# Picking the first four experts' rows inside gate and up of expert 0 in a transformer block with 64 experts

## The reference

```python
N_GROUPS, EXPERTS_PER_GROUP, TOP_K_EXPERTS = 8, 8, 2
D_EXPERT = D_MODEL // 8                       # 256
def hier_moe(h, wg, bg, we, be, w_gate, w_up, w_down):
    ...
    g_prob = jax.nn.softmax((xt @ wg).astype(jnp.float32) + bg.astype(jnp.float32), axis=-1)
    g_p, g_idx = lax.top_k(g_prob, 1)
    ...
    e_in = jnp.take_along_axis(e_logits, g_idx[:, :, None], axis=1)[:, 0]
    e_val, e_loc = lax.top_k(e_in, TOP_K_EXPERTS)
    weight = (g_p * jax.nn.softmax(e_val, axis=-1)).astype(h.dtype)
    ...
    def expert_chunk(args):
        xc, e = args
        return (jax.nn.silu(xc @ w_gate[e]) * (xc @ w_up[e])) @ w_down[e]
```

## Time and profile before

| | before |
|---|---|
| median of three runs | 1948.68 us |
| profiled execution | 1948.38 us |
| its span | 1946.6 us |
| TensorE busy | 1871.2 us (96%) |
| VectorE busy | 705.6 us (36%) |
| ScalarE busy | 584.6 us (30%) |
| GpSimd busy | 245.3 us (13%) |
| HBM read | 495.88 MB |

### The profile page before, as it was taken

One profiled execution on the slowest core, in us unless ns is written; L12 is line 12 of the kernel. 1 busy time (PEld: TensorE's weight loads), 2 busy tenths in 40 slices (PEclk: granted clock), 3 DMA queues, 4 the chain that ended last, 5 costly groups with the idle time before them and its releaser, 6 DMA issues.

```text
span 1946.6 us, 28605 instructions
## 1 busy us (share of the span) xinstructions
PE 1871.2 (96%) x11936; PEld 1352.2 (69%) x11936; DVE 705.6 (36%) x1773; ACT 584.6 (30%) x1212; POOL 245.3 (13%) x208
## 2 busy tenths in 40 slices
PE   6999999999999999999999999989999899999997
PEld 6887777777777767788986666556665565656663
DVE  5331223333766668701042232322323222222222
ACT  5323333333443444422312232212212122121322
POOL 2433343433000000144100000000000000000000
PEclk9999999999999999999999999999999999999999
DMA  9554233234232232145489999999999999999995
GB/s 284 134 147 118 66 86 82 70 71 92 45 76 44 55 117 79 44 142 195 191 349 420 429 426 426 427 427 427 427 426 427 427 428 426 428 427 427 427 423 231
DMA packets 177745, 505.95 MB, mean 260 GB/s; under 512 B 52930, under 2 KB 136258, under 8 KB 151754
## 3 DMA queue, kind: packets, MB, share of 16 engines
q1 hardware_dynamic: 175306, 495.66, 66.5%
q0 software_dynamic: 2304, 8.39, 1.1%
HBM read 495.88 MB, written 16.53 MB: 263 GB/s over the span
## 4 chain that ended last, share of the span: by engine, by line
PE 81%; DMA 16%; ACT 1%; DVE 1%; issue 0%; SPq 0%; POOL 0%; POOLq 0%; ACTq 0%; DVEq 0%
PE banks L967 26%; PE banks L1375 13%; PE banks L1124 9%; PE banks L1400 8%; DMA x_region<-in_w_up 7%; DMA at_region<-in_w_up 7%; PE banks L1297 6%; PE banks L1376 3%; PE banks L1104 3%; PE banks L1076 2%; PE banks L1054 2%; PE banks L1346 2%; DMA ht_region<-in_w_up 2%; PE banks L1016 1%; PE banks L1215 1%; PE banks L1061 1%
## 5 line engine op out<-in xcount | busy, mean ns | idle before, releaser
L967 PE MATMUL banks<-ht_rounded,ring_rounded 128*128 128x512 f32 x1056 | 359.2, 394 | 0.7 <-ACT at_region L1538 0.7
L967 PEld LDWEIGHTS banks<-ht_rounded,ring_rounded 128*128 128x128 f32 x1056 | 195.1, 188 | 53.3 <-issue 13.8
L1375 PE MATMUL banks<-at_region,ht_region 128*64 128x256 f32 x800 | 179.0, 382 | 9.3 <-DMA at_region<-in_w_up 9.3
L864 POOL TENSOR_TENSOR ring_rounded<-ring_region,at_rounded 128x512 fp32r<-128x512 f32 (+1 forms) x92 | 115.9, 1291 | 511.3 <-ACT at_rounded L1477 511.3
L1376 PE MATMUL banks<-at_region,ht_region 128*64 128x256 f32 x768 | 175.3, 388 | 0.0
L2269 DVE SCALAR_TENSOR_TENSOR at_rounded<-banks,small,ring_rounded 128x512 fp32r<-128x512 f32 x128 | 96.1, 751 | 208.8 <-ACT ring_rounded L1763 207.9
L1763 ACT ACTIVATE ring_rounded<-banks,small 128x512 fp32r<-128x512 f32 x128 | 88.0, 687 | 241.3 <-PE banks L1400 241.3
L2262 DVE COPY consts<-banks 128x128 f32<-128x128 f32 x64 | 18.7, 292 | 388.1 <-PE banks L1385 388.1
L1375 PEld LDWEIGHTS banks<-at_region,ht_region 128*64 128x64 f32 x800 | 109.1, 138 | 67.3 <-issue 21.1
L967 PE MATMUL banks<-ht_rounded,at_rounded 128*128 128x512 f32 x352 | 142.7, 405 | 1.0 <-ACT at_region L1530 0.7
L1753 ACT ACTIVATE ring_region<-banks,consts 64x256 f32<-64x256 f32 x64 | 30.0, 469 | 364.4 <-PE banks L1376 364.1
(11 more groups left out here) (300 smaller groups left out, 3488.2 us busy)
## 6 DMA issues: line engine op xcount, KB each, us to landing
at_region<-in_w_gate SPq DMA_DIRECT2D x23, 2048.0 KB, 30.0
at_region<-in_w_up SPq DMA_DIRECT2D x22, 2048.0 KB, 27.6
at_region<-in_w_down SPq DMA_DIRECT2D x22, 2048.0 KB, 23.9
ring_region<-in_w_in SPq DMA_DIRECT2D x36, 1024.0 KB, 5.9
x_region<-in_w_down SPq DMA_DIRECT2D x17, 2048.0 KB, 26.6
x_region<-in_w_up SPq DMA_DIRECT2D x15, 2048.0 KB, 28.9
x_region<-in_w_gate SPq DMA_DIRECT2D x14, 2048.0 KB, 29.9
ring_region<-in_w_gate SPq DMA_DIRECT2D x9, 2048.0 KB, 32.6
```

What stands on the lines that cost most here:

```text
L864: ins = nc.gpsimd.tensor_tensor(w_low[n % RING][:, ks, 0:width], ring[n % RING][:, ks, 0:width], w_high[n % 2][:, ks, 0:width].bitcast(F32 ...
L967: ins = mm(out, w[:, k, 0:width], h[:, k, :], start=k == 0 and i == 0, stop=k == KT - 1 and i == 2)
L1375: mm(place[0:CAP, 0:D_EXPERT], x, gate[j], start=j == 0, stop=j == KT - 1)
```

## The change

- **Fillers**: 7, 1 and 2 products in place of 16, 4 and 6.
- **Pick matrix**: the half for experts 0 to 3 is built first, by itself, and signals a semaphore of its own, `first_picks`; then the half for experts 4 to 7 (`pick_ready`).
- **Picks**: four of the sixteen picks of the first half stand ahead of expert 0; pick j + 4 then stands ahead of gate and up of slice j. The four banks are 6, 2, 3 and 0, since bank 7 now takes gate and up of expert 0 at the same time.
- **Root products** of group 0 move from ahead of gate and up of expert 0 to behind them, ahead of `gu_done`.
- The copies on ScalarE and VectorE keep their order and count (`copy_first`). `FIRST_PARTS` has a single part, so `FIRST_MORE` is 0, and all later counts stay as they were.

```diff
+FIRST_PARTS = ((0, HALF),)
+FIRST_MORE = len(FIRST_PARTS) - 1
...
-        def half_places(g, h):
-            return (whole_banks if h or g else first_banks, TURN4)
+        first_places = ((banks[:, 6, :], banks[:, 2, :], banks[:, 3, :], banks[:, 0, :]), (banks[:, 2, :], banks[:, 3, :], banks[:, 0, :]))
...
             place_rows(0)
-            keep_busy(16)
+            keep_busy(7)
             pe.wait_ge(chosen_ready, 1)
...
-            keep_busy(4)
+            keep_busy(1)
             place_slots(0)
-            keep_busy(6)
+            keep_busy(2)
+
+            first_rows = xg[0].rearrange("r (p k) -> r k p", k=KT)
+
+            def pick_first(part, j):
+                lo, hi = FIRST_PARTS[part]
+                if j == 0:
+                    pe.wait_ge(first_picks, part + 1)
+                if part == 0 and j == 0:
+                    pe.wait_ge(idx_ready, 1)
+                    pe.wait_ge(xg_in[0], 16)
+                places = first_places[part]
+                at = j - len(places)
+                if at >= 0:
+                    pe.wait_ge(xT_v if at % 2 else xT_a, part * KT // 2 + at // 2 + 1)
+                mm(places[j % len(places)][:, 0:hi - lo], first_rows[:, j, :], pick[:, lo:hi], start=True, stop=True).then_inc(picked, 1)
...
-                if picks is not None:
+                if picks is not None and (g or e8 >= PER // 2):
                     i = max(j for j in range(KT) if TURN4[j] == 1)
                     pe.wait_ge(xT_v if i % 2 else xT_a, done + i // 2 + 1)
                 fence(c, g)
-                if e8 == 0:
+                def root_of_slots():
...
+                if e8 == 0 and not begins_all(c, g):
+                    root_of_slots()
                 for j in range(KT):
                     if picks is not None:
                         pe.wait_ge(xT_v if j % 2 else xT_a, done + j // 2 + 1)
...
+                    if begins_all(c, g) and e8 == 0 and j + len(first_places[0]) < KT:
+                        pick_first(0, j + len(first_places[0]))
...
+                if e8 == 0 and begins_all(c, g):
+                    pe.wait_ge(pick_ready, 1)
+                    ins = root_of_slots()
                 ins.then_inc(gu_done, 1)
...
-            pick_half(0, 0)
+            for j in range(len(first_places[0])):
+                pick_first(0, j)
...
-            build_pick(0, 0)
+            v.tensor_copy(group_slots, slot_of_row[:, 0:PER]).then_inc(own_slots, 1)
+            dve.wait_ge(own_slots, 1)
+            pick_by_slots = pick.rearrange("p (e s) -> p e s", e=PER)
+            for lo, hi in FIRST_PARTS:
+                es = slice(lo // CAP, hi // CAP)
+                v.tensor_tensor(pick_by_slots[:, es, :], bcast(iota, 1, es.stop - es.start),
+                                bcast(group_slots[:, es], 2, CAP), ALU.is_equal).then_inc(first_picks, 1)
+            es = slice(HALF // CAP, PER)
+            v.tensor_tensor(pick_by_slots[:, es, :], bcast(iota, 1, PER - es.start), bcast(group_slots[:, es], 2, CAP),
+                            ALU.is_equal).then_inc(pick_ready, 1)
```

More of the change, by code:

```diff
@@ L553, in picks_ahead, with half_after @@
         def picks_ahead(c, g):
-            return g * 2 * KT if fast(c) else (c * N_GROUPS + g) * KT + N_GROUPS * KT
+            return g * 2 * KT + (FIRST_MORE * KT if g else 0) if fast(c) else (c * N_GROUPS + g) * KT + N_GROUPS * KT + FIRST_MORE * KT
         def copies_ahead(c, g):
-            return g * KT if fast(c) else (c * N_GROUPS + g) * (KT // 2) + N_GROUPS * KT // 2
+            return g * KT + (FIRST_MORE * KT // 2 if g else 0) if fast(c) else ((c * N_GROUPS + g) * (KT // 2) + N_GROUPS * KT // 2
+                                                                               + FIRST_MORE * KT // 2)
+        def half_after(g, h):
+            return h * (KT // 2) + (FIRST_MORE * KT // 2 if h and not g else 0)
         def begins_all(c, g):
@@ L1279, in pick_half @@
             def pick_half(g, h):
                 pe.wait_ge(pick_ready, g + 1)
-                pe.wait_ge(idx_ready, 1)
-                pe.wait_ge(xg_in[g % 2], g // 2 * 16 + 16)
-                place, turn = half_places(g, h)
                 rows = xg[g % 2].rearrange("r (p k) -> r k p", k=KT)
+                if not h:
+                    pe.wait_ge(xg_in[g % 2], g // 2 * 16 + 16)
                 for j in range(KT):
-                    if (h or g) and j == TURN4.index(0):
+                    if j == TURN4.index(0):
@@ L1294, in pick_half @@
                     if i is not None:
-                        pe.wait_ge(xT_v if i % 2 else xT_a, copies_ahead(0, g) + h * 8 + i // 2 + 1)
+                        pe.wait_ge(xT_v if i % 2 else xT_a, copies_ahead(0, g) + half_after(g, h) + i // 2 + 1)
                     slots = pick[:, h * HALF:(h + 1) * HALF]
-                    mm(place[turn[j]][:, 0:HALF], rows[:, j, :], slots, start=True, stop=True).then_inc(picked, 1)
+                    mm(whole_banks[TURN4[j]][:, 0:HALF], rows[:, j, :], slots, start=True, stop=True).then_inc(picked, 1)
@@ L1356, in gate_up @@
                 picks = e8 // (PER // 2) if fast(c) and e8 % (PER // 2) == 0 else None
-                done = copies_ahead(c, g) + (picks or 0) * (KT // 2)
+                done = copies_ahead(c, g)
+                if picks:
+                    done += half_after(g, picks)
+                if begins_all(c, g) and any(e8 * CAP == lo for lo, _ in FIRST_PARTS[1:]):
+                    picks, done = -1, KT // 2
                 if e8 == 0 and not fast(c):
@@ L1423, in group @@
                     if begins_all(c, g) and e8 == 0:
+                        for part in range(1, len(FIRST_PARTS)):
+                            for j in range(KT):
+                                pick_first(part, j)
                         place_marks(c)
@@ L1729, in copy_half, with copy_first @@
             def copy_half(g, h):
[L1730 removed]
                 for j in range(0, KT, 2):
[L1732 to L1733 removed]
+                    act.wait_ge(picked, picks_ahead(0, g) + 2 * half_after(g, h) + j + 1)
+                    fn(xT[:, 0, j, :], whole_banks[TURN4[j]][:, 0:HALF], ACT.Copy, scale=ln2_sb[:, j:j + 1]).then_inc(xT_a, 1)
+            def copy_first(part):
+                lo, hi = FIRST_PARTS[part]
+                for j in range(0, KT, 2):
+                    act.wait_ge(picked, part * KT + j + 1)
+                    fn(xT[:, 0, j, lo:hi], first_places[part][j % len(first_places[part])][:, 0:hi - lo], ACT.Copy, scale=ln2_sb[:, j:j + 1]).then_inc(xT_a, 1)
             def square_rows(c, g, b):
@@ L1790, in _ @@
             fn(r_tmp[:, 4], r_tmp[:, 3], ACT.Exp).then_inc(e_exped, 1)
-            copy_half(0, 0)
+            for part in range(len(FIRST_PARTS)):
+                copy_first(part)
             for g in range(N_GROUPS):
```

25 lines of the change are left out of this document (16 added, 9 removed).

## The result

The changed kernel takes 1959.2 us in the median of six runs (1957.36 to 1960.25), against 1948.14 us for the kernel before in six runs: a ratio of 1.0054 (95% interval 1.0044 to 1.0064), so some 10.5 us slower by the ratio and 11.1 us by the medians. The forecast was 1950.7 us in a range of 1946.8 to 1953.8 us. The sign of the sum was right, the call of no measurable change (0.72) was wrong, and the time lies outside the range.

The account below looks back on a forecast made before the run. The end was taken to hang on TensorE's time at expert 4's loads, 1053.67 us, before unbroken DMA reading. The profiled 1948.38 us plus 2.0 gave 1950.4; with 0.3 for the runs' median, 1950.7 us, range 1946.8 to 1953.8 us.

Parts of the forecast that it names:

- The sign of the sum: Whole kernel: forecast slower, by 2.0 us against the profiled 1948.38 us.
- the call of no measurable change: Whole kernel: time stays within 0.2%, 3.9 us, of before; chance 0.72.
- What bounds the kernel: TensorE's time at expert 4's loads, 1053.67 us, sets the end; shifts at 1001.74 us reach it one for one.
- filled hole: DMA hole from 996 to 1005 us: mostly filled, no gain forecast; rival that 4.4 us is saved, 1944.3 us, chance 0.08.
- The weave: Picks between expert 0's gate and up pairs: 0.12 us switching a slice, twelve slices 12.0 us, 0.3 us gained after roots.
- the upper bound of 0.24: Most that switching between pick and pair may cost a slice: four times the 0.06 us read between gate records.
- The rule weighed against the row: Skill page's rule that weight loads overlap only across row groups, 2.6 us more, set against gate records 0.21 us apart.
- Fillers and start of the picks: Ahead of expert 0: fewer fillers and a half pick matrix start the picks at 984.85 instead of 986.47 us, 1.6 us gained.
- The clock's fall: Rival: half clock under the picks from 980.5 us, 1952.4 us; again after the marks' wait, 1954.0 us; chance 0.27.
- The new wait: TensorE ahead of place_marks waits 2.3 us for VectorE; marks start at 1003.7 instead of 1001.74 us, 2.0 us lost.

Follow-up runs that it names:

- e6_probe: Kernel before plus test products: twelve full-width in a block, full-width ones woven into expert 1, half-width into expert 2; 1961.12 us, ratio 1.0067.
- e7_half_picks: Changed kernel with each woven pick split in two products of 64 weight columns, one per column half; 1951.49 us, ratio 1.0014.
- e8: Changed kernel with woven picks split in column halves, place_marks behind gate and up of expert 1, and 12, 3 and 3 fillers; 1948.91 us, ratio 1.0002.
- e9: Changed kernel with its sixteen picks in one block ahead of expert 0 and 12, 3 and 3 fillers; 1947.85 us, ratio 0.9995.
- e2: Changed kernel with the 16, 4 and 6 fillers of before put back; 1956.64 us, ratio 1.0043.
- e1: Changed kernel with its sixteen picks in one block ahead of expert 0 again, few fillers kept; 1949.81 us, ratio 1.0008.
- e4: Changed kernel with the woven picks two at a time, ahead of every second slice; 1955.23 us, ratio 1.0038.
- e5: Changed kernel with place_marks behind gate and up of expert 1 and VectorE's marks reading behind expert 0's hidden values; 1955.74 us, ratio 1.0033.

## Why the prediction was wrong

**What bounds the kernel: right.** The end followed TensorE's time at expert 4 in ten kernels, and nothing that was won for the DMA queue before it counted. This also decided the "filled hole" rival.

**The weave, "I take 0.12 us, twice the row": wrong, and the main error.** The switch there and back costs 0.44 us a slice, nearly twice even the upper bound of 0.24. Over the eleven slices ahead of the last pick that is 11 x 0.32 = 3.5 us more than forecast. The bound was four times a gap of 0.06 us read on entering gate and up after a pick. But that gap is between two gate records and says nothing of the time from the pick to the first gate record, where most of the cost lies (0.29 us in the weave). The row was not of the thing priced. The gap of 0.23 us in the kernel before's own load rows at 1046.50 us, which marks this change, was left out of the reckoning. e6_probe and e7_half_picks show what it is: in these runs a product adds only its own time when the one ahead has the same width in the array (full after full, half after half), and more when the width changes.

**The rule weighed against the row: I gave it too little.** The Trainium skill's rule, page "TensorE: Matmul & The Clock Gate", section "Part 3: Packing small matmuls — row/col tiling", warned of bare loads. By it 2.6 us would have been added, and the runs showed 12 x 0.44 = 5.3 us. As worded (only different row groups overlap) it does not agree with the runs either: half-width products on all rows overlapped wholly in e6_probe (0.65 us a slice). The measurement decides, and it goes by the columns' width.

**Fillers and start of the picks, 1.6 us gained: wrong by the clock.** Only 0.56 us was gained, since the chain ran at half clock: `place_slots` took 1.97 us instead of 1.00. With a full clock the forecast start held to 0.1 us (e8, e9, with 18 fillers), but in part by luck. The prediction let the gathered rows hold the start at 12.09; in e8 and e9 SyncE's load behind the same transfer goes out at 11.68 and 11.59 us, and the pick matrix on VectorE is what the picks wait for (0.26 us). Nor was the gain mostly the fillers': at full clock 26 of them cost only 0.35 us more (e2), and 1.36 of the 1.71 us between before and e8 lie between before and e2, which has the same number of fillers, a clock that stayed up, and the pick matrix by halves. The prediction saw the clock's fall in before but did not price it here.

**The clock's fall, a rival at 0.27: it came.** It came in the profiled execution of every kernel with 7, 1 and 2 fillers (the changed one, e1, e4, e5 and e7). In the changed kernel it came earlier than the rival had it, by 979 us instead of 980.5. The price was reckoned as 1.5 to 1.7 us under the picks and the same again after the wait for the marks. Measured against e2_fillers, it is 1.89 and 1.38 us. The sum agrees, but the first part in a way by luck: 1.09 us of it are the picks, and 0.80 us the later start, which the rival did not have. The rival's whole time, 1954.0 us, was short mainly because it stood on the same cheap weave (3.5 us), and by the later start of the picks (1.06 us against the forecast).

**The new wait: right in place and size.** 2.3 us forecast, 2.07 us measured; e5 shows that it is on the path.

**The filled hole: "the change fills most of it" was wrong, and cost nothing.** The slow slices held back the quarter loads, and the hole stayed at 242 GB/s. That filling it brings nothing was right (e8 against e9).

The sum, at the load of expert 4: 2.0 forecast, 3.5 more for the weave, 1.06 for the later start of the picks, about 1.1 for the first picks at half clock and 1.35 for the marks' slow products make 9.0 us; 8.93 were measured.

## What to carry to other kernels

Before weaving two streams of products on TensorE, look at the width of their weights. If one uses the whole array and the other its column halves, each change costs, here 0.34 us (128 columns moving) to 0.44 us (256) for 32-bit floats there and back; splitting the wide product in two halves removed the cost at once. Where a row is taken to price an operation, check that it spans the whole interval that the operation would lengthen, from the last record of the one kind to the first of the other.

A hole in the DMA stream is worth filling only if no later wait of the queue holds the same time: find the last hole before the unbroken stretch first.

## What the runs showed of the hardware

- TensorE's records stay "busy" across the change of width: in the weave it is busy for 9.00 of 9.00 us from 996 to 1005 us, though a slice of 1.32 us holds 0.88 us of work. The gap shows only in the weight loads' rows, as "issue".
- The clock did not go by the number of fillers alone. With 10 of them it was 0.50 from 979 to 988 us in the changed kernel, and it fell in the profiled executions of all five kernels that had 10. With 26 it was 0.50 from 978 to 981 us in the kernel before, 0.52 from 979 to 981 us in e6_probe, and did not fall in e2_fillers. With 18 (12, 3 and 3) it stayed at 2.4 GHz in both kernels that had them, in one profiled execution each, so whether that always holds is open. A wait of 2.07 us behind small products was followed by another fall in the changed kernel; one of 2.08 us in e2, 2.07 in e4 and 2.23 in e7 was not, so this fall is not settled by the wait's length.
